# One matmul of a slab a few columns wider, and the slabs behind tables in one region

## The reference, cut to what matters

```python
# layers 0 and 1
h = rms_norm(x, g_pre_mix[l]) * (1 + scale_a) + shift_a
y = token_mixer(h, w_in[l], ..., w_out[l])          # w_in: 2048 x about 4600
x = x + gate_a * rms_norm(y, g_post_mix[l])
h = rms_norm(x, g_pre_mlp[l]) * (1 + scale_m) + shift_m
x = x + gate_m * rms_norm(square(relu(h @ w_up[l])) @ w_down[l], g_post_mlp[l])   # 2048 x 8192 x 2048
# S5 layer
u, z = split(rmsnorm(h, g_pre) @ s5_w_in)           # z is the gate product
y = gelu(s5_ssm(u, ...))
y = y * sigmoid(y @ w_glu + b_glu) * silu(z)
h = h + rmsnorm(y @ s5_w_out, g_post)
# then k, v, forget gates, and the FoX layer
```

## Time and profile before

| | |
|---|---|
| three runs, us | 3144.55, 3145.53, 3142.89 (median 3144.55) |
| profiled execution: span from first to last instruction | 3145.5 us |
| profiled execution: its own time | not recorded apart from its span |
| TensorE, matmuls | 3075.0 us, 98% of the span, 26577 instructions |
| TensorE, weight loads | 2931.5 us, 93% |
| VectorE | 2404.3 us, 76% |
| ScalarE | 1529.5 us, 49% |
| TensorE's mean granted clock | 0.992 of full speed |

### The profile page before, as it was taken

One profiled execution on the slowest core, in us unless ns is written; L12 is line 12 of the kernel. 1 busy time (PEld: TensorE's weight loads), 2 busy tenths in 40 slices (PEclk: granted clock), 3 DMA queues, 4 the chain that ended last, 5 costly groups with the idle time before them and its releaser, 6 DMA issues.

```text
span 3145.5 us, 61783 instructions
## 1 busy us (share of the span) xinstructions
PE 3075.0 (98%) x26577; PEld 2931.5 (93%) x26577; DVE 2404.3 (76%) x2964; ACT 1529.5 (49%) x2232; POOL 0.2 (0%) x4
## 2 busy tenths in 40 slices
PE   5999999999999999999999999999999999999999
PEld 3889999999999988989999999999899999999998
DVE  7898999788888788776887666687688767556764
ACT  2465664343434556666534444445433556434454
POOL 0000000000000000000000000000000000000000
PEclk7999999999999999999999999999999999999999
DMA  9888869999999745665688666895555554654453
GB/s 409 337 301 331 318 254 349 346 334 350 337 339 342 254 163 212 218 225 175 231 298 307 221 223 240 283 303 202 217 181 189 215 190 158 213 179 159 148 188 121
DMA packets 137025, 791.05 MB, mean 251 GB/s; under 512 B 20081, under 2 KB 38641, under 8 KB 46001
## 3 DMA queue, kind: packets, MB, share of 16 engines
q1 hardware_dynamic: 119714, 769.33, 67.2%
q10 hardware_dynamic: 17040, 17.76, 1.6%
HBM read 769.28 MB, written 17.76 MB: 250 GB/s over the span
## 4 chain that ended last, share of the span: by engine, by line
PE 53%; DVE 2%; ACT 1%; issue 0%; ACTq 0%; DVEq 0%
PE bk L436 52%; DVE wl L1649 1%; PE bk L440 0%; ACT wh L949 0%; DVE pr L1649 0%; DVE Hst L1649 0%; DVE xl L1649 0%; DVE ss L1649 0%; DVE qa L1657 0%; DVE p L1649 0%; DVE X L1649 0%; DVE raw L1657 0%; ACT ln L949 0%; DVE hg L1657 0%; ACT rsy L949 0%
## 5 line engine op out<-in xcount | busy, mean ns | idle before, releaser
L1649 DVE TENSOR_TENSOR wl<-raw,wh 128x2048 fp32r<-128x2048 f32 (+1 forms) x481 | 1092.5, 2271 | 321.1 <-ACT wh L949 318.1
L436 PE MATMUL bk<-HX,wh 128*128 128x256 f32 (+1 forms) x8058 | 1105.8, 294 | 1.8 <-ACT wh L949 1.6
L949 ACT ACTIVATE wh<-raw 128x2048 fp32r<-128x2048 f32 x477 | 911.8, 1912 | 351.1 <-PE bk L436 322.7
L436 PEld LDWEIGHTS bk<-HX,wh 128*128 128x128 f32 x8058 | 1022.2, 188 | 53.4 <-ACT wh L949 2.4
L436 PE MATMUL bk<-HX,wl 128*128 128x256 f32 x4560 | 569.0, 277 | 5.2 <-DVE wl L1649 5.2
L436 PEld LDWEIGHTS bk<-HX,wl 128*128 128x128 f32 x4560 | 542.3, 188 | 7.1 <-DVE wl L1649 7.0
L436 PE MATMUL bk<-hb,wh 128*128 128x256 f32 (+1 forms) x3916 | 488.0, 282 | 0.1
L436 PEld LDWEIGHTS bk<-hb,wh 128*128 128x128 f32 x3916 | 468.2, 188 | 8.2 <-issue 0.3
L1657 DVE SCALAR_TENSOR_TENSOR raw<-raw,cb 128x2048 f32<-128x2048 f32 x192 | 437.5, 2283 | 14.8 <-DMA raw<-in_w_ada 14.7
L436 PE MATMUL bk<-hb,wl 128*128 128x256 f32 x2048 | 253.8, 276 | 0.0
L436 PEld LDWEIGHTS bk<-hb,wl 128*128 128x128 f32 x2048 | 242.5, 188 | 0.0
(11 more groups left out here) (313 smaller groups left out, 2584.1 us busy)
## 6 DMA issues: line engine op xcount, KB each, us to landing
raw<-in_w_ada SPq DMA_DIRECT2D x192, 1024.0 KB, 6.9
raw<-in_w_up SPq DMA_DIRECT2D x128, 1024.0 KB, 6.5
raw<-in_w_down SPq DMA_DIRECT2D x128, 1024.0 KB, 5.7
raw<-in_w_in SPq DMA_DIRECT2D x66, 1024.0 KB, 5.3
raw<-in_kv_w SPq DMA_DIRECT2D x33, 1024.0 KB, 4.9
raw<-in_w_out SPq DMA_DIRECT2D x32, 1024.0 KB, 5.4
raw<-in_s_w_in SPq DMA_DIRECT2D x32, 1024.0 KB, 4.9
raw<-in_fox_w_in SPq DMA_DIRECT2D x32, 1024.0 KB, 4.8
```

The lines of the kernel that those rows point to most:

```text
L436: return e.matmul(o_, l_, r_, start=start, stop=stop, skip_group_check=True)
L949: return e.activation(o_, i_, f, **kw)
L1649: return e.tensor_tensor(o_, a_, b_, op)
```

## The change

One matmul of certain one-region slabs gets `more` columns: the first one of the fifth tile (q = 4, part 0). It starts at the same column of x high and reads `more` columns on, into x low, and it writes as many columns of the second half of its bank. In a one-region slab nobody reads them. The widths are 4 to 116 in slabs 8 to 36 of the first w_in (4 more for each slab), 4 to 48 and 20 to 130 in the first and second slab behind each of the 12 table groups, and 72 to 168 in slabs 6 to 14 of the gate product. Widths that fall on a slab which is not one-region have no effect.

The 24 slabs behind the 12 table groups leave `IN_TWO`, so that they become one-region. The two behind place 22 stay two-half.

```diff
-          | {J_MLP[1] + _m + _i for _m in TABLES for _i in (1, 2)}
+          | {J_MLP[1] + TABLES[0] + _i for _i in (1, 2)}
...
+WIDER = {_n: 4 * (_n - 7) for _n in range(8, 37)}
+WIDER.update({J_MLP[1] + _m + _i: (4 if _i == 1 else 10) * (_u + 1) + 10 * (_i - 1) for _u, _m in enumerate(TABLES[1:]) for _i in (1, 2)})
+WIDER.update({J_Z + _n: 12 * _n for _n in range(6, 15)})
...
-            def high_times(bank, wh, x, q, one=False):
+            def high_times(bank, wh, x, q, one=False, more=0):
                 if q in WIDE and not one:
                     mm(bank[:, :], wh, x.rearrange("p a t -> p (a t)"), q == 0, False)
                 else:
+                    both = x.rearrange("p a t -> p (a t)")
                     for part in range(2):
-                        mm(bank[:, 0:T], wh, x[:, part, :], q == 0 and part == 0, False)
+                        n = T + (more if q == 4 and part == 0 else 0)
+                        mm(bank[:, 0:n], wh, both[:, T * part:T * part + n], q == 0 and part == 0, False)
...
-                    high_times(bank, WH[w][:, k, :], x(k), q, one)
+                    high_times(bank, WH[w][:, k, :], x(k), q, one, WIDER.get(j, 0) if one else 0)
```

## The result

The changed kernel takes 3159.40 us (median of four runs, 3158.21 to 3161.53), the kernel before 3143.72 us (median of four, 3141.47 to 3145.53). The ratio is 1.0049, with a 95% interval of 1.0037 to 1.0062: 15.7 us slower, more than the 0.2% that can be told from no change, and above the range of the prediction. The profiled execution of the changed kernel took 3158.78 us, and its span is 3157.0 us, 11.5 above that of the earlier trace rows.

The account below looks back on a forecast made before the run. TensorE, busy 3075.0 of 3145.5 us, was taken as the bound, through the time between matmuls. Tables +2.1, gate product -0.1 and first w_in -0.4 sum to +1.6 on 3144.55: 3146.2 us, range 3140.0 to 3153.0 (8 in 10).

Parts of the forecast that it names:

- How often a single matmul of 256 + w columns ends the slow pace.: All widened slabs: the one unknown the sum hangs on, taken as 0.4 for each widened matmul, bounds never and always.
- rival 1: Slow pace stays in all 45 slabs behind the tables: 7.1 us there, +8.3 to +8.6 in all, 3153.0 us; chance 0.2.
- Once fast, I take it to stay fast until the next interruption.: Widened slabs: a fast pace, once reached, lasts until small matmuls or a wait; each further slab behind the tables gains 0.08.
- Two halves to one region: 24 slabs behind the tables: one region saves 0.04 us per slab in the fast pace, costs 0.17 in the slow.
- Columns: Three stretches, 3488 more columns at 0.417 ns: 1.45 us at most (0.58 first w_in, 0.50 tables, 0.37 gate product).
- Gate product, first w_in: Net of pace gained and columns paid: -0.1 us in the gate product, -0.4 in the first w_in, half kept for VectorE waits.
- It ... adds no instruction or transfer.: The widened ninth matmul of a slab: waits for nothing new and adds no instruction or transfer; nothing costed for it.
- tables: Slabs behind the 12 table groups: +1.6 us from the paces and +0.5 for columns, +2.1 in all.

## Why the prediction was wrong

**"How often a single matmul of 256 + w columns ends the slow pace."** I took 0.4 from the three-matmul groups. Behind the tables of the changed kernel it ended the slow pace in no slab, in the run with large widths in two. In the first w_in three of 24 slabs show a fast low part with the widths, and four in the profile without any. The price of the step is the distance from +1.6 to rival 1's 7.1, 5.5 us.

**"Once fast, I take it to stay fast until the next interruption."** This is the step that failed as a mechanism. The memory of the pace is real, the durations of the earlier trace rows were read rightly, but a longer matmul is itself one of the things that begin the slow pace. 43 of 48 and 42 of 48 widened matmuls did it to a fast slab in the two runs with a row of widths, and three of three behind the tables of the changed kernel. I had excluded it by what the groups of three do in the earlier trace rows, and three is the very length that does no harm. The kernel before shows groups of three only, so its trace couldn't tell.

**Two halves to one region.** Rival 1 was right, in mechanism and size: it gave 7.1 us for slabs that stay slow behind the tables, and the profile without widths has 7.35. What I had as the case against it, that most groups ended it at the fourth, was weak, for in the earlier trace rows it is the second two-half slab that ends it, and the change takes that slab away. The rule that the loss always comes is not true either. One profile has the same code at +0.9.

**Columns.** 0.42 ns each, 0.50 us forecast behind the tables, 0.38 measured; in the gate product 0.37, compatible with +0.59 less slab 391.

**Gate product, first w_in.** -0.1 and -0.4 forecast; +0.59, and nothing that can be told. Both small, both on the losing side, for the same reason.

**"It ... adds no instruction or transfer."** True for the widened matmul. For the 24 slabs put in one region the prediction counted 18 matmuls for nine and priced their columns and their distance, but not that they are 432 more instructions to be fetched. That shifted the fetch of the pieces so that one fell into the 64 small matmuls, behind six 1 MB loads. It cost 7.17 us, shown by taking 432 instructions out elsewhere (32.35 to 25.05 us). By the windows of the stretch, 5.1 us of this is idle time, from the two stops of 3.66 and 2.04 us (none and 0.25 before), and 2.0 is busy time, most of it at half clock: the high part at 6.07 instead of 4.92 in TensorE's row.

So +1.6 became +15.5: tables 7.7 for 2.1, gate product 0.6 for -0.1, w_in about 0 for -0.4, and 7.2 for an edit costed at nothing. Rival 1 with the missing 7.2 would have been 3160.

The back-to-back distance of 256-column matmuls was 113.3 or 117.8 ns in every stretch that I read, also in the 15 experiments. The Trainium skill (TensorE: Matmul & The Clock Gate, section "Back-to-back issue gap") gives N/2.4 + 2.5 ns, 109.2 here, for the isolated gap of a matmul alone, and says that in a stream of weight loads and matmuls, which this is, both set the distance. The prediction had left this second half out. An estimate by the formula for the slabs behind the tables is 1.0 us, the columns and 216 more gaps of 2.5 ns, where 7.7 were lost.

**What stays open.** What makes the cycle of three; what in the widths 52, 60 and 76 does no harm; what decides the pace in which TensorE comes out of a table group, since with one-region slabs behind it came out slow behind 33 of 36 groups in three profiles and fast behind 9 of 12 in a fourth; which run lengths end the slow pace when a slab is entered slow (those that did so in the one run came in pairs, 3 and 4, 9 and 10, 15 and 16, then 6 and 7, 12 and 13); and why a remainder of 66 is better at the GLU start than 48. That TensorE stands for pieces is shown by the ends of its stops, and that their place decides by the exchange of 24 slabs. That a piece waits behind the loads is shown only in part. With the loads issued later the stop shrank and the clock held, in one run, but the fetch itself has no row that says what it waited for.

## What to carry to other kernels

- Where TensorE is the bound at 98%, look at the distance between equal matmuls before anything else, and by place. 4% between two paces is invisible in busy shares and in the list of waits, and the durations of one line show it at once (276 against 279 ns). A few longer matmuls among short ones can set the pace of hundreds that follow; in this kernel they did no harm in runs of three, and that can be tried in one run.
- Count the instructions of an edit, not only their time. Where small matmuls outrun the fetch, the place of the 16 KB pieces decides, and an edit moves it for everything behind it. After an edit that changes the number of instructions, look for new idle time put down to "issue" far from the edit, and balance the length before judging the edit itself. A block of large loads issued just ahead of such a place made it worse: without it the stretch was 4.0 us shorter, in one run.
- A forecast that rests on a behaviour for which the trace has examples of one kind only (here groups of three) should give the other outcome more than a fifth.

## What the runs showed of the hardware

- Matmuls of 256 columns with a new weight tile each follow each other in 113.3 or in 117.8 ns, at the same granted clock of 1.00, and keep to it for dozens of slabs. From the faster, runs of 3, 6, 9, 12 and 15 matmuls of 512 columns kept it in 7 of 7 and other lengths from 1 to 16 lost it in 17 of 17. The 512-column ones in such a run repeat 388, 392 and 394 ns, and the fast pace follows a 394.
- TensorE's instructions come in pieces of 16 KB, about 256 each. At one place of small matmuls the stretch took 24.8 to 32.4 us, by where in a piece it began. Its stops end 2.2 to 2.9 us after the record of a piece begins. The longest was 4.2 us in the kernel without widths; the 3.7 us of the changed kernel went with a clock at the 1.2 GHz level for 6.8 us.
